# A one-core decoder block: order of loads at two stage starts, and the lead of the own expert fetches

## What is computed

```python
q = (h @ w_pq).reshape(B, S, 8, 2, 128)
s = einsum('bshjd,hjnd->bshjn', q, sub_keys)
v1, i1 = top_k(s[..., 0, :], 16); v2, i2 = top_k(s[..., 1, :], 16)
top_s, pos = top_k(v1[..., None] + v2[..., None, :], 16)   # over 256 sums
idx = (i1 * 128 + i2) at pos;  gate = softmax(top_s)
a = einsum('tkd,td->tk', expert_u[idx], h)
y = einsum('tk,tkd->td', gate * gelu(a), expert_v[idx])    # 8 x 16 experts a token
x = x + gt2 * rmsnorm(y, g_post_ffn)
```

## Time and profile before

| what | value |
|---|---|
| median of 3 runs (lowest, highest) | 1783.82 us (1779.32, 1789.91) |
| the profiled execution's own time | 1788.98 us |
| its span | 1787.2 us |
| mean granted TensorE clock | 0.982 of full speed |
| busy share of the span: PE, DVE, ACT, POOL | 96%, 73%, 42%, 29% |
| stage_rest, PE's first and last matmul | 956.0 and 1242.4 us |
| stage_experts with its first tile, PE's first and last matmul | 1242.7 and 1777.3 us |

### The profile page before, as it was taken

How to read it: one execution, slowest core, us unless ns; L and a number is a source line. 1 busy time by engine, 2 the same in 40 slices (tenths; PEclk the granted TensorE clock), 3 DMA queues, 4 the chain that set the end, 5 groups by cost and what they waited for, 6 DMA issues and landing times. The chain is left out here.

```text
span 1787.2 us, 22493 instructions
## 1 busy us (share of the span) xinstructions
PE 1708.3 (96%) x7869; PEld 1411.2 (79%) x7869; DVE 1311.3 (73%) x2200; ACT 758.6 (42%) x1261; POOL 524.9 (29%) x423
## 2 busy tenths in 40 slices
PE   6999896989999999999998999999999999999997
PEld 5877675778877778888886888888788888888786
DVE  5787776559999969999994333333578868787878
ACT  5225344343322367777773222232333333333333
POOL 1000001115667610000000000000767668667750
PEclk9999998989999999999999999999999999999999
DMA  9563001332144435765667665553898999898985
GB/s 381 214 244 108 1 1 43 147 130 80 62 136 141 139 132 171 217 211 190 204 217 247 214 207 183 176 176 110 307 343 308 329 330 335 314 326 322 335 326 224
DMA packets 160415, 369.96 MB, mean 207 GB/s; under 512 B 16608, under 2 KB 78560, under 8 KB 157024
## 3 DMA queue, kind: packets, MB, share of 16 engines
q1 hardware_dynamic: 137824, 302.08, 48.5%
q0 software_dynamic: 22528, 67.19, 10.7%
HBM read 306.30 MB, written 62.91 MB: 207 GB/s over the span
## 5 line engine op out<-in xcount | busy, mean ns | idle before, releaser
L2022 PE MATMUL banks<-hl,actT 128*128 128x512 f32 x2268 | 518.3, 391 | 7.4 <-DVE actT L2244 7.3
L2022 PEld LDWEIGHTS banks<-hl,actT 128*128 128x128 f32 x2268 | 427.3, 189 | 98.1 <-DVE hl L2239 8.9
L1997 PE MATMUL banks<-actT,hl 128*128 128x512 f32 x1224 | 280.1, 391 | 7.0 <-ACT kept_acts L1931 6.7
L2154 POOL DMA_INDIRECT rows<-in_v,own_index x65 | 86.5, 1331 | 675.0 <-POOLq L1856 608.8
L1814 PE MATMUL banks<-actT,hl 128*128 128x512 f32 x1176 | 275.9, 390 | 1.8 <-PEq L1351 1.8
L1997 PEld LDWEIGHTS banks<-actT,hl 128*128 128x128 f32 x1224 | 231.2, 189 | 56.0 <-issue 7.8
L1814 PEld LDWEIGHTS banks<-actT,hl 128*128 128x128 f32 x1176 | 217.7, 188 | 45.3 <-issue 2.2
L2197 ACT ACTIVATE hl<-v_raw 128x1024 fp32r<-128x1024 f32 x125 | 132.4, 1059 | 273.3 <-PE banks L2022 206.9
L1592 PE MATMUL banks<-actT,hl 128*128 128x512 f32 x1032 | 241.5, 392 | 6.3 <-POOL hl L1439 5.0
L1592 PEld LDWEIGHTS banks<-actT,hl 128*128 128x128 f32 x1032 | 191.5, 188 | 49.6 <-POOL hl L1439 5.9
L2239 DVE TENSOR_TENSOR hl<-v_raw,hl 128x1024 fp32r<-128x1024 f32 x125 | 153.2, 1226 | 77.6 <-ACT hl L2197 57.2
(11 more groups left out here) (274 smaller groups left out, 2173.2 us busy)
## 6 DMA issues: line engine op xcount, KB each, us to landing
raw<-in_u SPq DMA_DIRECT2D x128, 512.0 KB, 3.9
v_raw<-in_v SPq DMA_DIRECT2D x128, 512.0 KB
expert_gates<-gates SPq DMA_DIRECT2D x12, 2048.0 KB, 9.8
group_gates<-expert_gates SPq DMA_DIRECT2D x32, 768.0 KB
wada<-in_w_ada SPq DMA_DIRECT2D x10, 2048.0 KB, 8.3
acts_in<-early_activations SPq DMA_DIRECT2D x100, 192.0 KB
early_activations<-kept_acts SPq DMA_DIRECT2D x52, 256.0 KB, 2.2
early_activations<-gate_acts SPq DMA_DIRECT2D x48, 256.0 KB, 2.3
```

Of the source, the lines that this page charges most:

```text
L1997: last = nc.tensor.matmul(m.psum[u % 2][:], hl[:, x, u % m.split, kc * P:(kc + 1) * P], m.actT[:, z, kc, :], start=(kc == 0 and j == 0), s ...
L2022: last = nc.tensor.matmul(bank(m, t, half)[:], w[:, x, t * P:(t + 1) * P], m.hl[:, z, j, half * S:(half + 1) * S], start=(first and k == 0 ...
L2154: nc.gpsimd.indirect_dma_start(out=fetched[k % FETCH], out_offset=None, in_=rows_of_v, in_offset=bass.IndirectOffsetOnAxis(ap=m.own_index[ ...
```

## The change

In `stage_rest`, the raw tiles 4 and 5 are issued before the wait for the stored gates and the two gate loads; the first gates of `stage_experts` are loaded in `stage_rest`, once group 11 has been weighed and its buffer is free, and the buffer numbers of the later gate loads follow (`gate_buffer`); `acts_in` is loaded at n = 48 instead of behind the last store; `store` runs 8 tiles behind the raw loads rather than 6 (`LATE`); DVE weighs tiles 0 to 4 behind low(7) rather than tiles 0 to 2 behind low(5). In `stage_experts`, the own activations are fetched with a lead that grows from 17 to 25 slots over the first 16 slots, over three semaphores rather than two; and own rows begin at program place 12, spread over 116 places.

```diff
+LATE = 8
@@ stage_rest, SP
-            for k in range(2):
-                sp.wait_ge(m.stored[k], 16 * GATE_PAIRS)
-            for u in range(RAW):
-                sp.wait_ge(acts_stored[u], 16 * stored_before)
-            load_gates(0)
-            load_gates(1)
-            for u in range(2):
-                sp.wait_ge(m.early_stored[u], 16 * EARLY // 2)
-            for n in range(RAW, count + RAW + 2):
+            for n in range(RAW, count + LATE):
+                if n == RAW + 2:
+                    for k in range(2):
+                        sp.wait_ge(m.stored[k], 16 * GATE_PAIRS)
+                    for u in range(RAW):
+                        sp.wait_ge(acts_stored[u], 16 * stored_before)
+                    load_gates(0)
+                    load_gates(1)
+                    for u in range(2):
+                        sp.wait_ge(m.early_stored[u], 16 * EARLY // 2)
...
-                if n >= RAW + 2:
-                    store(n - RAW - 2)
+                if n >= LATE:
+                    store(n - LATE)
                 if n % JG == 3 and 2 <= n // JG < count // JG:
                     load_gates(n // JG)
-            for j in range(JG):
-                sp.dma_start(m.acts_in[:, j, :], a.early[TILES[JG + j], :, 0:SD]).then_inc(m.acts_landed[j], 16)
+                if n == count - JG:
+                    for j in range(JG):
+                        sp.dma_start(m.acts_in[:, j, :], a.early[TILES[JG + j], :, 0:SD]
+                                     ).then_inc(m.acts_landed[j], 16)
+                if n - LATE == count - JG - 1:
+                    free = (count // JG - 2) % 2
+                    sp.dma_start(gates[:, free].rearrange("p b j t -> p (b j t)"),
+                                 a.gates[:, SEQUENCE[1][0] * size:(SEQUENCE[1][0] + 1) * size]
+                                 ).then_inc(gates_landed[free], 16)
@@ stage_rest, DVE
-                if n == 3:
-                    weigh(0)
-                    weigh(1)
-                if n >= 3:
+                if n == CLEAR:
+                    for k in range(CLEAR - 1):
+                        weigh(k)
+                if n >= CLEAR:
                     weigh(n - 1)
@@ stage_experts
-        act_landed = [sem("own_act_landed0"), sem("own_act_landed1")]
+        act_landed = [sem(f"own_act_landed{i}") for i in range(3)]
-        first_row = 8
+        first_row = 12
+        def gate_buffer(q):
+            return (rest_groups + q) % 2
@@ stage_experts, SP
-                if s < GROUPS and kinds[s] == "plain":
+                if 2 <= s < GROUPS and kinds[s] == "plain":
                     load_gates(s)
@@ stage_experts, POOL
-                    ).then_inc(act_landed[k // CHUNK_K % 2], 16)
+                    ).then_inc(act_landed[k // CHUNK_K % 3], 16)
+            def ahead(k):
+                return min(SLOTS, k + 1 + CHUNK_K + min(FETCH + 2, k // 2))
...
-                    if c < chunks - 1:
-                        fetch_act(k + CHUNK_K)
+                    for q in range(ahead(k - 1) if k else CHUNK_K, ahead(k)):
+                        fetch_act(q)
```

More of the change, by code:

```diff
@@ L2123, in load_gates @@
                 q = plain_before(s * JG) // JG
+                b = gate_buffer(q)
                 if q >= 2:
@@ L2126, in load_gates @@
                 at = SEQUENCE[s][0] * size
-                sp.dma_start(gates[:, q % 2].rearrange("p b j t -> p (b j t)"), a.gates[:, at:at + size]
-                             ).then_inc(gates_landed[q % 2], 16)
+                sp.dma_start(gates[:, b].rearrange("p b j t -> p (b j t)"), a.gates[:, at:at + size]
+                             ).then_inc(gates_landed[b], 16)
             for s in range(GROUPS + 1):
-                if s < GROUPS and kinds[s] == "plain":
+                if 2 <= s < GROUPS and kinds[s] == "plain":
                     load_gates(s)
@@ L2226, in weigh @@
                 q = i // JG
+                b = gate_buffer(q)
                 if j == 0:
-                    dve.wait_ge(gates_landed[q % 2], ((rest_groups + 1 - q % 2) // 2 + q // 2 + 1) * 16)
+                    dve.wait_ge(gates_landed[b], ((rest_groups + 1 - b) // 2 + q // 2 + 1) * 16)
                 dve.wait_ge(acts_landed[j], (loads_before(n) + 1) * 16)
@@ L2232, in weigh @@
                 V.tensor_tensor(weighed[:, i % 3, :].rearrange("p (b t) -> p b t", t=TB),
-                                acts[:, j, :].rearrange("p (b t) -> p b t", t=TB), gates[:, q % 2, :, j, :],
+                                acts[:, j, :].rearrange("p (b t) -> p b t", t=TB), gates[:, b, :, j, :],
                                 ALU.mult).then_inc(weighed_done, 1)
@@ L2247, in weigh_own @@
             def weigh_own(c):
-                dve.wait_ge(act_landed[c % 2], 16 * CHUNK_K * (c // 2 + 1))
+                dve.wait_ge(act_landed[c % 3], 16 * CHUNK_K * (c // 3 + 1))
                 ks = slice(c * CHUNK_K, (c + 1) * CHUNK_K)
```

## The result

Over 20 runs each, the changed kernel has a median of 1775.40 us and the kernel before one of 1788.22; the ratio is 0.9934, with a 95% interval from 0.9919 to 0.9948. So it is faster by 0.66%, some 11.8 us; the two medians by themselves are 12.8 us apart. The forecast was 17.2 us, from 1783.82 to 1766.6. Two things are off, and by the medians they are of one size: the gain is 4.4 us smaller (about a third by the ratio, a quarter by the medians), and the 1783.82 us, a median of three runs, lay 4.4 us under the median of twenty. The profiled execution of the changed kernel has 1772.7 us, 2.7 us under its own median, and a span of 1770.9. It is 16.3 us shorter than the profiled execution of before, nearly what was forecast.

What follows compares the result with a forecast made beforehand. The prediction took PE, busy 96% of the span, as the bound, its pauses ending on DVE or ACT. Gains of 7.8 + 5.7 + 3.7 = 17.2 us took 1783.82 to 1766.6 us, range 1759 to 1776.

Steps and rivals of the forecast that it cites:

- Part 1: Head of stage_rest: raw tiles 4 and 5 ahead of the gates cut PE's 6.71 us pause and lower clock; gain 7.8 us.
- The Trainium skill's estimate: Head of stage_rest: raw tile 4 lands 3.2 us after the gate store, pause 2.4 us, sum 1.5 us smaller.
- Part 2: Start of stage_experts: gates loaded early remove PE's pause at place 3 and the lower clock behind it; gain 5.7 us.
- 3.18 + 2.5 = 5.7 us: Start of stage_experts: PE's 3.18 us pause at place 3 plus 2.5 us lost at the lower clock behind it.
- Part 3: Middle of stage_experts: longer fetch lead removes DVE's 41.3 us of waits and three PE pauses; gain 3.7 us (0 to 4.2).
- 1.14 + 1.08 + 1.94 = 4.16 us: Middle of stage_experts: three PE pauses to go with DVE's waits; 0.5 us left for new pauses, gain 3.7 us.
- I take the same difference from the median: Whole kernel: the 17.2 us gain is subtracted from the median of 1783.82 us, giving 1766.6 us.
- (a): Head of stage_rest: raw tile 4 lands late, pause 2.9 us and lower clock stays; 1770.6 us, chance 0.11.
- (b): stage_experts: `v` tiles become the wait, own-row gain lost and 3 us of pauses added; 1773.3 us, chance 0.14.
- (c): stage_experts: POOL becomes the bound with issues of 2.15 us, own rows end 30 us late; 1796.6 us, chance 0.04.
- the signs that I had named as proof: Both stages: no pause over 1.5 us near 967, clock 1.00, raw tile 4 by 966.5, no DVE waits for own activations.

Runs made afterwards that it cites:

- the paced one: The changed kernel with POOL's first 16 activation fetches paced, two to a `v` tile; ratio to the kernel before 0.9938, median 1774.28 us.
- the first profile of before: The kernel before, unchanged, in its first profiled execution, from which the prediction was made: 1788.98 us, stage_experts 535.0 us.
- the change again: The changed kernel run and profiled a second time, nothing altered; ratio to the kernel before 0.9938, median 1777.22 us.
- the last combination: The changed kernel with gelu(1) to gelu(3) ahead of hi(4) to hi(6) on ACT and own rows from place 8, not paced; ratio 0.9919, median 1771.35 us.
- the third profile of before: The kernel before, unchanged, profiled a third time; 1785.43 us in one run, stage_experts 529.0 us.
- the combination with pacing: The changed kernel with gelu(1) to gelu(3) ahead of hi(4) to hi(6) on ACT and POOL's first 16 activation fetches paced; ratio 0.9913, median 1771.28 us.
- the kernel with ACT's order alone: The kernel before with only gelu(1) to gelu(3) put ahead of the high parts of raw tiles 4 to 6 on ACT; ratio 0.9976, median 1782.24 us.

## Why the forecast was too large

**Part 1, right.** Forecast 7.8 us, measured 7.2 to 7.7 in the six profiles with it (stage_rest 279.0 to 279.5 against 286.7). The remaining pause was put at 0.9 us and is 1.24 to 1.70, since raw tile 4 is taken 1.8 to 2.2 us after SP is released by the store and not 1.4. The clock kept 1.00 as said. The Trainium skill's estimate ("DMA: Bandwidth & Descriptors", on the anatomy of one DMA on the GpSimd path) was 3.2 us for the same and a pause of 2.4; the trace has 2.04 and 1.49, between the two and a little nearer to my value. Gates and raw tile 6 came in time.

**Part 2, right in mechanism, wrong in size.** The pause at place 3 went, `v_raw` of place 4 was there in time, and the lower clock went. The step that failed is the term "3.18 + 2.5 = 5.7 us". It took both numbers from one execution. In the five profiles with that code the pause is 3.18, 2.19, 1.77, 1.70 and 3.27 us. Worked out as in the prediction, the lower clock cost 2.5, 1.6, nothing, nothing and 1.4 us behind them, so the term is 3.5 us in the mean, from 1.7 to 5.7; the first profile had a long pause and the dearest stretch at the lower clock. A gain of 0.5 us that was not seen is the border of the stages, 0.98 us before and 0.47 in all kernels with the early gates.

**Part 3, the same.** DVE's waits of 41.3 us went to nothing, DMA and POOL held. The failed term is "1.14 + 1.08 + 1.94 = 4.16 us": the waits of DVE are there in every profile of before (35 to 43 us), but what of them reaches PE is 4.2 us in the first profile and 1.2, 1.2, 0.8 and 0.9 in the other four with that code, 1.7 in the mean. I read it as what is left of 41 us after DVE's lead over PE has been used up, a small difference of two large numbers, and no row of one profile tells its spread. The two terms were 9.9 us in the forecast and are 5.2 in the mean. The new stops of the last section take some back: a stage_experts without any pause takes 523.2 us, and the changed kernel with the paced one 524.1 to 527.5, where the forecast left 0.5 us for new pauses.

**The base.** "I take the same difference from the median" carried the gain of one execution over to a median of three runs of 1783.82 us, and that median alone put the forecast time 4.4 us too low. The profile's 1788.98 us, which I had taken for long, is within 0.8 us of the median of twenty. The stretches of this code that the change does not touch vary too: stage_rest began between 956.0 us (the first profile of before) and 962.1 us (the second), behind the same code.

**The rivals.** (a) is excluded: no profile with the new load order shows 2.9 us or a lower clock near 970. (b) did not come as it was put: part 3 gave what of DVE's waits had reached PE, and behind 1281 us PE runs without a pause in all seven profiles with the longer lead, at 337 GB/s in the changed kernel. ACT's waits alone don't exclude it: with the unnamed ones they are 27.8 us in the first profile of the change but 45.3 in the second, against 40.0 before, and PE's stops near 1275 stand beside such waits. The rule of the Trainium skill ("DMA: Bandwidth & Descriptors", "Queues, rings and completion order"), that each DMA engine alternates between queues with work, is neither shown nor contradicted by these runs. (c) is excluded: POOL is busy 284.40 us in the middle stretch, less than before. Of the signs that I had named as proof, nearly all came out right in the first profile of the change (raw tile 4 was taken at 968.94, which is 966.9 on the scale of before, where stage_rest began 2.0 us earlier; I had said 966.5), and yet the size was wrong, because they test the mechanism and not the baseline.

## What to carry over

A pause that PE has because another engine's slack ran out differs from one execution to the next, so take its size from several profiles of the kernel before, and give its term a range from nothing up to what one profile shows; a pause that a fixed chain sets (here store, load, copy, activation: 6.4 to 6.7 us in five profiles) can be taken from one. Before a load is moved, look whether the waiting instruction needs it at all: here three pairs of instructions on ACT in the other order gave three quarters of part 1's gain. A wait that is removed from an engine which runs ahead counts only by what reaches the engine that is behind.

## What the runs showed that was not expected

Some 35 us into stage_experts PE stops for 1 to 2 us in the middle of a tile, with no releaser, in three profiles: the change again, the paced kernel and the last combination; with own rows from place 8 and in the third profile of before there are stops of 0.3 and 0.7 us of the kind. In the three the granted clock is lowered around it (0.81, 0.79 and 0.80 over 8 us each), although each stop is shorter than the 2.19 us pause at place 3 was. In all five an unnamed wait of ACT for `v_raw` ends within 3 us of a stop. These waits are of 7.8 us in the paced kernel and in both profiles of the change, and there are others further on without a stop. In that stretch the DMA engines are nearly idle (0.29 and 103 GB/s from 1266 to 1280), so a lack of bandwidth does not explain it. The single kernel without own activation fetches has neither, but the combination with pacing, which issues them all, has no stop either, and unnamed waits of 5.3 us at most. What makes these stops is open, and it is most of the spread of the changed kernel's stage_experts, 524.1 to 527.5 us.

The clock did not follow the length of a pause alone: after 1.94 us it kept 1.00 in the first profile of before, and after 1.82 us it was lowered to 0.76 over 7 us in the kernel with ACT's order alone. At place 3 it kept 1.00 after 1.77 us in the third profile of before and was lowered after 2.19 us in the second.
